# Mixer rounds with three weight slots: the third slot made by quarters in ticks 4 to 7

## The reference

```python
h = rms_norm_2(x, g_mix[i])
proj = h @ w_in[i]
glu_a, glu_b, q, k, v, z, a_in, b_in, gate_a, gate_b = split_cols(proj, IN_SIZES)
c = glu_a * jax.nn.sigmoid(glu_b)
c = depthwise_conv(c, conv_dw_w[i]) + conv_dw_b[i]
c = jax.nn.silu(layer_norm_2(c, conv_ln_g[i], conv_ln_b[i]))
y_conv = c @ w_conv_out[i]
qkv = jax.nn.silu(depthwise_conv(jnp.concatenate([q, k, v], axis=-1), qkv_conv_w[i]))
...
o_fwd = gated_delta_rule(q, k, v, g[:, :, 0], beta[:, :, 0])
o_bwd = rev(gated_delta_rule(rev(q), rev(k), rev(v), rev(g[:, :, 1]), rev(beta[:, :, 1])))
o = rms_norm_2(o_fwd + o_bwd, delta_norm_g[i]) * jax.nn.silu(z.reshape(bsz, t_len, N_HEADS, HEAD_DIM_2))
y_delta = o @ w_delta_out[i]
y = jax.nn.sigmoid(gate_a) * y_conv + jax.nn.sigmoid(gate_b) * y_delta
x = x + y @ w_o[i]
```

## Time and profile before

| | |
|---|---|
| time, median of 3 runs | 1209.02 us (1206.76 to 1209.89) |
| the profiled execution | 1204.78 us, its span 1203.0 us |
| PE busy (matmuls) | 1170.6 us, 97% |
| PE loading weights | 1087.1 us, 90% |
| DVE busy | 841.6 us, 70% |
| ACT busy | 701.7 us, 58% |
| POOL busy | 320.0 us, 27% |
| mean granted clock of PE | 0.997 |

### The profile page before, as it was taken

One profiled execution on the slowest core, in us unless ns is written; L12 is line 12 of the kernel. 1 busy time (PEld: TensorE's weight loads), 2 busy tenths in 40 slices (PEclk: granted clock), 3 DMA queues, 4 the chain that ended last, 5 costly groups with the idle time before them and its releaser, 6 DMA issues.

```text
span 1203.0 us, 21393 instructions
## 1 busy us (share of the span) xinstructions
PE 1170.6 (97%) x8616; PEld 1087.1 (90%) x8616; DVE 841.6 (70%) x1519; ACT 701.7 (58%) x1181; POOL 320.0 (27%) x257
## 2 busy tenths in 40 slices
PE   8999999999999999999999999999999999999997
PEld 7777899998877799998889999998989989999886
DVE  6796588884675579885568787888954565555456
ACT  5475576663458566664366667766667445444344
POOL 1172200000016300000166666575555320000000
PEclk9999999999999999999999999999999999999999
DMA  7633355556553356555343332332222646555542
GB/s 285 252 140 140 123 211 206 184 181 219 175 191 125 129 208 219 196 208 210 128 160 126 121 115 105 133 114 98 94 83 106 227 170 224 210 183 203 202 155 81
DMA packets 31587, 199.74 MB, mean 166 GB/s; under 512 B 4289, under 2 KB 6481, under 8 KB 8706
## 3 DMA queue, kind: packets, MB, share of 16 engines
q1 hardware_dynamic: 29506, 189.27, 43.6%
q0 software_dynamic: 1840, 8.60, 1.9%
q10 hardware_dynamic: 144, 0.52, 0.1%
HBM read 197.33 MB, written 1.05 MB: 165 GB/s over the span
## 4 chain that ended last, share of the span: by engine, by line
PE 83%; DVE 8%; ACT 4%; issue 2%; POOL 1%; DMA 0%; SPq 0%; POOLq 0%; DVEq 0%; ACTq 0%
PE ps L1182 24%; PE ps L1183 23%; PE ps L1184 23%; PE ps L1559 1%; PE ps L1575 1%; DVE ps L2824 1%; DVE wlo L2370 1%; PE ps L1336 1%; DVE conv L2755 1%; PE ps L1355 1%; PE ps L1323 1%; PE ps L1189 1%; PE ps L1207 1%; DVE halves L2472 1%; PE ps L1276 1%
## 5 line engine op out<-in xcount | busy, mean ns | idle before, releaser
L1182 PE MATMUL ps<-halves,whi 128*128 128x256 f32 x1472 | 409.8, 278 | 0.2
L1184 PE MATMUL ps<-halves,wlo 128*128 128x256 f32 x1472 | 404.8, 275 | 0.0
L1183 PE MATMUL ps<-halves,whi 128*128 128x256 f32 x1472 | 404.8, 275 | 0.0
L2370 DVE TENSOR_TENSOR wlo<-raw,whi 128x2048 fp32r<-128x2048 f32 (+1 forms) x133 | 301.3, 2268 | 112.2 <-ACT whi L1839 108.7
L1839 ACT ACTIVATE whi<-raw 128x2048 fp32r<-128x2048 f32 (+1 forms) x143 | 269.5, 1887 | 102.4 <-PE ps L1184 96.3
L1182 PEld LDWEIGHTS ps<-halves,whi 128*128 128x128 f32 x1472 | 282.5, 192 | 0.8 <-DVE halves L2963 0.5
L1184 PEld LDWEIGHTS ps<-halves,wlo 128*128 128x128 f32 x1472 | 282.6, 192 | 0.0
L1183 PEld LDWEIGHTS ps<-halves,whi 128*128 128x128 f32 x1472 | 282.5, 192 | 0.1
L1106 POOL TENSOR_TENSOR wlo<-raw,whi 128x1024 fp32r<-128x1024 f32 x72 | 172.5, 2404 | 51.0 <-ACT whi L1848 50.4
L1000 POOL TENSOR_TENSOR rstd<-sumsq,half_power 128x1 f32<-128x1 f32 x14 | 11.3, 809 | 573.3 <-ACT xn L1866 406.0
L1182 PE MATMUL ps<-whi,halves 128*128 128x512 f32 (+4 forms) x440 | 148.2, 337 | 4.8 <-DVE halves L2472 4.0
(11 more groups left out here) (337 smaller groups left out, 1849.5 us busy)
## 6 DMA issues: line engine op xcount, KB each, us to landing
raw<-in_stream SPq DMA_DIRECT2D x176, 1024.0 KB, 4.8
gain<-in_gains POOLq DMA_DIRECT2D x7, 512.0 KB, 5.7
bias<-in_rel POOLq DMA_DIRECT2D x1, 1536.0 KB, 8.6
raw<-in_stream SPq DMA_DIRECT2D x2, 648.0 KB, 7.3
cst<-in_consts POOLq DMA_DIRECT2D x1, 1280.5 KB, 5.9
raw<-in_stream SPq DMA_DIRECT2D x2, 528.0 KB, 4.2
x<-in_x SPq DMA_DIRECT2D x2, 512.0 KB, 4.3
out<-xn SPq DMA_DIRECT2D x4, 256.0 KB, 2.5
```

The lines of the kernel that those rows point to most:

```text
L1182: nc.tensor.matmul(out, a_hi, b_hi, start=start, stop=False)
L1183: nc.tensor.matmul(out, a_hi, b_lo, start=False, stop=False)
L1184: return nc.tensor.matmul(out, a_lo, b_hi, start=False, stop=stop)
L2370: dve.tensor_tensor(used(wlo, n), used(raw, n), used(whi, n).bitcast(F32), ALU.subtract)\
```

## The change

In rounds with three slots the third one is made by quarters in ticks 4, 5, 6 and 7, one in each, instead of by halves in ticks 4 and 5. In ticks 4 to 6 the quarter stands behind the level step (where part 1 stood), in tick 7 ahead of the query products and behind the check (where part 0 stood). The halves of the slot two ahead are rounded and split in ticks 4 and 6. The slot is evacuated in tick 0 of the next round instead of in tick 6. `TAP_COUNT`, the fillers and all other waits stay.

```diff
--- before.py
+++ after.py
@@ -567,14 +567,38 @@
 ORDINAL_OF_CONV = {key: n for n, key in enumerate(CONVS)}
 
 
+SPREAD_FROM = 4
+EARLY_QUARTERS = {7}
+
+
+def spread(r, i):
+
+    return len(ROUNDS[r]) == 3 and i >= SPREAD_FROM
+
+
 def slot_at(r, i):
 
-    return ROUNDS[r][i // 2][0] if i // 2 < len(ROUNDS[r]) else None
+    return ROUNDS[r][2 if spread(r, i) else i // 2][0]
+
+
+def quarters(r, i, late):
+
+    if not spread(r, i):
+        return [(i % 2, late)]
+    q = i - SPREAD_FROM
+    return [(q // 2, q % 2)] if late != (i in EARLY_QUARTERS) else []
+
+
+def split_at(r, i):
+
+    if not spread(r, i):
+        return i % 2
+    return None if i % 2 else (i - SPREAD_FROM) // 2
 
 
 def finished_slot(r, i):
 
-    if i % 2 or r + i == 0:
+    if i % 2 or r + i == 0 or (i > SPREAD_FROM and spread(r, i)):
         return None
     return slot_at(r, i - 1) if i else slot_at(r - 1, TICKS - 1)
 
@@ -1136,8 +1160,8 @@
                         pool.wait_ge(*S["conv_var"].at())
                         pool.tensor_tensor(conv_rsd[:, :], conv_rsd[:, :], half_power[:, 0:TT], ALU.pow)\
                             .then_inc(*S["conv_rstd"].one())
-                    if slot_at(r, i):
-                        split_half(slot_of[slot_at(r, i)] + AHEAD, i % 2)
+                    if split_at(r, i) is not None:
+                        split_half(slot_of[slot_at(r, i)] + AHEAD, split_at(r, i))
 
 
             load_gain(6)
@@ -1775,14 +1799,14 @@
                     if r == 0 and i == 4:
                         decay_sums()
                     level_first(r - 1, i)
-                    if slot_at(r, i):
-                        half_slot(slot_at(r, i), i % 2, 0)
+                    for m, part in quarters(r, i, 0):
+                        half_slot(slot_at(r, i), m, part)
                     chain_first(r - 2, i)
                     if i == 7:
                         query_products(r)
                     level_second(r - 1, i)
-                    if slot_at(r, i):
-                        half_slot(slot_at(r, i), i % 2, 1)
+                    for m, part in quarters(r, i, 1):
+                        half_slot(slot_at(r, i), m, part)
                     chain_second(r - 2, i)
                     prepare(r, i)
                     if r == 8:
```

## The result

The changed kernel takes 1215.53 us (median of 16 runs), the kernel before 1207.6 us on the same chips (16 runs). The ratio is 1.0051, with a 95% interval of 1.0039 to 1.0063: slower by 6.1 us (4.7 to 7.6). It is not the quotient of the two medians, which lie 7.9 us apart. The profiled execution takes 1209.51 us, with a span of 1207.7 us against 1203.0, and a mean granted clock of 0.997 as before. It is the fastest of the 16: the five runs at 0.996 or 0.997 take 1209.5 to 1211.8 us, the eleven at 0.990 to 0.993 take 1213.1 to 1216.9.

A forecast was written before the change was run, and what follows sets the result against it. PE, busy nearly all of the span, was taken to bound the kernel, with DVE nearly as full. Terms 0.2 + 1.3 + 0.2 + 3.6 + 0.4 = 5.7 us on 1209.02 gave 1214.7 us, range 1210.5 to 1218.5 (own forecast 1211.5 to 1217).

The forecast's parts named there:

- Step 4: Tick 4 of rounds 5 to 7: nothing won; PE waits 1.56 us for DVE's join 4 instead of running a quarter.
- Step 5: Rounds 5 and 7: can start 1.3 us earlier; round 6: cannot, since join 5 stands behind DVE's v-slot evacuation.
- Tick 6 of round 6: Quarter behind step 6 makes the sums (L1516) 1.34 to 1.5 us late; DVE is full, so +1.3 us, once.
- Tick 7: Early quarter delays query products and correction by 1.34 us, mostly covered by PE's waits; +0.2 us each in rounds 5 and 7.
- Round 8: Last gates slot read after the early quarter; ACT's rounding, DVE's remainders and residual delay the correction: +3.6 us.
- The lower bound: Round 8's correction delayed only by the plain PE order, with 1.98 us of fillers: +2.7 us.
- Round 9: Tick 0: moved evacuation, 0.58 us on ACT, stands ahead of values L1645 needs, with 0.19 in hand: +0.4 us.
- The sum: Whole kernel: 0.2 + 1.3 + 0.2 + 3.6 + 0.4 = 5.7 us slower, with bounds 2.5 to 6.4 us.
- The waits of before: PE's waits before the change: all for products of the head's chain, none for weights, 0.8 us at most each.
- The rival of the clock: New idle pieces lower PE's clock once or twice in rounds 6 to 8: +7.4 to +9.1 us in all; chance 0.12.
- The rival "faster": Shorter queues before steps 4 and 5 move steps 4 to 6 up: at most 3.7 us gained, 1205.3; chance 0.10.

## Why the prediction was right, point by point

- **Step 4.** Right: the quarter in front of it was replaced by a wait of 1.32 us behind the same join, in rounds 5, 6 and 7. The run with the moved taps shows that DVE's queue was what held it.
- **Step 5.** Right in rounds 5 and 7 (1.3 us earlier) and in round 6 (held by the v slot, wait 1.98). What the prediction did not see is how close a second holder stood. It gave step 5 of round 7 a margin of 0.65 us behind join 5 (871.03 against 871.68), but ACT's copy of the inverse (L2142, 870.48, 1.11 us long) ended at 871.59 there. In the changed kernel that copy ends 0.15 us before step 5 of round 7 (872.28, 872.43), and in round 5 join 5, behind ACT's tanh of the second slot, ends 0.06 us before it (804.98, 805.04). So neither cost anything in the change; as soon as join 4 was freed, both did.
- **Tick 6 of round 6.** +1.3 forecast, +1.19 measured, and it was not taken up in round 7.
- **Tick 7.** Right in the number: rounds 5 and 7 cost 0.17 and 0.16 us, the waits at the round's edge having covered the rest. It is not the early quarter's alone: the sums already come 0.21 and 0.19 us late in the round (25.02 against 24.81, 26.05 against 25.86 us), and POOL's product ends 0.09 us before L1565 (883.74, 883.83). PE's order and POOL arrive together, and no run parts them. The kernel with one quarter moved turned this into a gain.
- **Round 8.** +3.6 forecast, +3.44 and +3.45 measured, by the chain that was forecast: from rounding to correction it is 2.65 us (917.26 to 919.91), forecast 2.66. The lower bound, +2.7 by plain order, was 0.4 too high. It took the 1.98 us of the second fillers in the earlier trace rows as PE's own; they take 1.71, and the rest was a wait for the residual already before the change, as was 0.1 us behind each of the first fillers and the check.
- **Round 9.** +0.4 forecast, +0.34 measured, with a wait of 0.22 us on ACT's values.
- **The sum.** 5.7 forecast, 5.3 in the profile at full clock, 6.1 (4.7 to 7.6) in the runs. In the three groups of experiments, runs of the kernel before with a mean granted clock of 0.997 take 1204.5 to 1204.9 us, those of the changed kernel (in its first 16) 1209.5 to 1210.3, so 4.6 to 5.8 apart. That the median of 1215.53 us came so near the forecast 1214.7 is partly luck: it was built on 1209.02, the median of three runs, where 16 gave 1207.6, and this surplus hid most of the 2.2 us by which the medians moved further than 5.7.
- **The waits of before.** Not all were for the head's chain, as the prediction had it: one of 0.7 us was for POOL's `conv_rsd` in round 8. It did not move (0.6), so no term suffers.
- **The rival of the clock** was priced at 1.7 us for each fall and given 0.12 as something that would come on top. It is partly true: in round 6 the clock falls in some executions, for 1.66 us (36.55 against 34.89). The argument against it, that each gap is followed by 3 us of matmuls, overlooked round 6, where 2.5 us of them stand between a wait of 1.3 us and one of 2.0.
- **The rival "faster"** said that it decides at join 4. It does not decide there alone: with join 4 freed by 1.2 us, the sums of round 5 came at the same 25.02 us into the round. The rival would have needed ACT's queue too.
- The Trainium skill (Perfetto Trace Analysis, Identifying the Most-Contended Engine) judges PE's head-room by the busy share of the weight loads. In rounds 5 to 8 that leaves 132.20 - 121.86 = 10.3 us, and it bore on none of this: the kernel with one quarter moved got 2.4 us out of rounds 5 to 8 by the profile, and the place of the wait decided how much, not the size of the idle sum.

## What to carry to other kernels

Before independent work is taken away in front of a dependent step to fill a hole elsewhere, look at what releases that step: if another engine's queue ends just as the work does, the work was free there and is paid for wherever it goes. Move only the piece whose step is released by the engine you relieve, here one quarter in two rounds, not four in four. And follow the last read of a moved piece of work: here it released a buffer, and an engine that waited for the buffer stood in line ahead of the critical chain.

## What the runs showed of the hardware

- The clock of PE can fall after waits that are short one by one. In round 6, with waits of 1.3 and 2.0 us and 2.5 us of matmuls between them (PE busy 3.70 of 7 us), the clock fell to the lower level for 3.4 us in one profiled execution of the changed kernel and not in the other.
- In round 8 of the kernel with the quarter ahead of the check, the clock fell behind a wait of 1.49 us in front of step 5 (906.50): the granted clock is 0.75 in the stretch 905 to 910, and the matmuls of the quarter there start 0.21 us apart instead of 0.11. Most of it cost nothing, since it lay in the wait in front of step 6, which starts 27.51 us into the round, as in the kernel before (910.50 - 882.99). What reached into step 6 cost 0.4 us (0.88 against 0.50). So a lower clock cost time here only where PE held the path.
- The stretch behind the last feed-forward part of the second layer (596 to 616) has a granted clock of 0.91 in the profile of before and between 0.76 and 0.91 in those of the other kernels, whose code there is the same: 3.6 to 9.6 us at the lower level (20 x 0.09 x 2 and 20 x 0.24 x 2). That is 1.8 to 4.8 us lost, up to 3.0 more in one execution than in another. The two profiles of the changed kernel enter round 5 at 785.03 and 790.56 us, 5.5 apart, as much as the change itself costs. So a profile of one execution can't stand for the median.
- Sixteen filler matmuls in the wait of 2.0 us of round 6 delayed nothing (34.93 against 34.97 us).
